# A hybrid transformer block on one core: two rows of inverse roots by transfers through DRAM instead of TensorE

## What is computed

```python
def rms_norm(x, g):
    xf = x.astype(jnp.float32)
    y = xf * lax.rsqrt(jnp.mean(xf * xf, axis=-1, keepdims=True) + EPS)
    return (y * g.astype(jnp.float32)).astype(x.dtype)

h = rms_norm(x, norm_mix_g[l])          # the input of the mixer
parts = jnp.split(h @ w_in, ...)        # all projections of the mixer
...
o = o * lax.rsqrt(jnp.mean(o * o, axis=-1, keepdims=True) + EPS) * norm_g    # end of the gated recurrence
```

## Time and profile before

| what | value |
|---|---|
| median of 3 runs | 923.76 us (923.7 to 924.11) |
| the profiled execution | 923.25 us, of which the span of the trace is 921.5 us |
| PE busy | 911.4 us, 99% of the span |
| DVE busy | 627.7 us, 68% |
| ACT busy | 404.8 us, 44% |
| POOL busy | 99.6 us, 11% |

### The profile page before, as it was taken

How to read it: one execution, slowest core, us unless ns; L and a number is a source line. 1 busy time by engine, 2 the same in 40 slices (tenths; PEclk the granted TensorE clock), 3 DMA queues, 4 the chain that set the end, 5 groups by cost and what they waited for, 6 DMA issues and landing times.

```text
span 921.5 us, 11738 instructions
## 1 busy us (share of the span) xinstructions
PE 911.4 (99%) x4590; PEld 757.4 (82%) x4590; DVE 627.7 (68%) x753; ACT 404.8 (44%) x472; POOL 99.6 (11%) x116
## 2 busy tenths in 40 slices
PE   8999999999999999999999999999999999999997
PEld 6888888888888888888888978888888888888886
DVE  6887654654778475656545758688777777777796
ACT  6463311331455532443344547433333433455674
POOL 0024342300322000000021004000000000000002
PEclk9999999999999999999999999999999999999999
DMA  7568899224798728433223224333355433255563
GB/s 219 184 159 241 226 245 237 80 71 103 181 224 201 194 80 209 124 102 125 92 99 130 70 70 138 91 92 91 91 142 139 129 91 91 91 173 201 185 200 143
DMA packets 137478, 132.48 MB, mean 144 GB/s; under 512 B 6651, under 2 KB 115295, under 8 KB 137183
## 3 DMA queue, kind: packets, MB, share of 16 engines
q1 hardware_dynamic: 127438, 108.62, 39.6%
q0 software_dynamic: 9856, 23.07, 11.5%
q10 hardware_dynamic: 144, 0.26, 0.1%
HBM read 122.23 MB, written 25.17 MB: 160 GB/s over the span
## 4 chain that ended last, share of the span: by engine, by line
PE 93%; DVE 4%; ACT 2%; DMA 0%; issue 0%; SPq 0%; DVEq 0%; ACTq 0%
PE ps L685 71%; PE ps L1210 6%; PE ps L1222 5%; PE ps L1086 5%; PE ps L739 1%; PE ps L1114 1%; DVE wL L1655 1%; DVE hgF L1655 1%; DMA xtok<-in_x 0%; PE ps L929 0%; ACT hgF L1262 0%; PE ps L895 0%; PE ps L855 0%; DVE hgG L1848 0%; PE ps L915 0%
## 5 line engine op out<-in xcount | busy, mean ns | idle before, releaser
L685 PE MATMUL ps<-hH,wH 128*128 128x512 f32 x784 | 307.9, 393 | 2.1 <-DVE wL L1655 1.2
L685 PE MATMUL ps<-hH,wL 128*128 128x512 f32 x784 | 305.2, 389 | 0.0
L685 PE MATMUL ps<-hL,wH 128*128 128x512 f32 x784 | 305.2, 389 | 0.0
L1655 DVE TENSOR_TENSOR wL<-raw,wH 128x2048 fp32r<-128x2048 f32 (+3 forms) x119 | 209.6, 1769 | 59.9 <-ACT wH L1262 59.7
L1262 ACT ACTIVATE wH<-raw 128x2048 fp32r<-128x2048 f32 (+3 forms) x119 | 176.0, 1488 | 136.6 <-PE ps L685 128.5
L685 PEld LDWEIGHTS ps<-hH,wH 128*128 128x128 f32 x784 | 147.2, 188 | 35.0 <-DVE wL L1655 2.6
L685 PEld LDWEIGHTS ps<-hH,wL 128*128 128x128 f32 x784 | 147.1, 188 | 31.0
L685 PEld LDWEIGHTS ps<-hL,wH 128*128 128x128 f32 x784 | 147.2, 188 | 29.7 <-issue 0.2
L1262 ACT ACTIVATE ca<-za,par 128x512 f32<-128x512 f32 x22 | 18.0, 818 | 100.4 <-DVE za L1655 100.4
L1662 DVE SCALAR_TENSOR_TENSOR ca<-za,par,ca 128x512 f32<-128x512 f32 x44 | 33.1, 752 | 25.6 <-ACT ca L1262 23.4
L1662 DVE SCALAR_TENSOR_TENSOR cu<-zu,par,cu 128x512 f32<-128x512 f32 x44 | 33.1, 752 | 25.5 <-ACT cu L1262 23.4
(11 more groups left out here) (326 smaller groups left out, 1449.1 us busy)
## 6 DMA issues: line engine op xcount, KB each, us to landing
raw<-in_w_in SPq DMA_DIRECT2D x57, 512.0 KB, 4.8
raw<-in_w_up SPq DMA_DIRECT2D x44, 512.0 KB, 4.9
t<-in_w_down POOLq DMA_DIRECT2D x66, 256.0 KB, 5.0
raw<-t SPq DMA_DIRECT2D x11, 768.0 KB, 4.7
raw<-in_w_branch SPq DMA_DIRECT2D x24, 256.0 KB, 4.8
t<-t POOLq DMA_DIRECT2D x22, 256.0 KB, 9.9
raw<-in_w_down SPq DMA_DIRECT2D x10, 512.0 KB, 4.2
raw<-in_w_out SPq DMA_DIRECT2D x8, 512.0 KB, 4.2
```

The costliest lines, as they stand in the source:

```text
L685: last = pe.matmul(out_ap, a, b, start=start and k + m == 0, stop=stop and m == 2 and k == len(terms) - 1)
L1655: q.sig(dve.tensor_tensor(out_ap, a, b, op), sem)
```

## The change

The two `rows_of` jobs on PE are gone. In their place POOL writes the small tile to a buffer `rows_dram` in DRAM, token by token, waits for that transfer, and reads the 512 numbers back as a row for all 128 partitions: `rstd` to `rstd_row`, and `statr` to a new tile `hgrow`. DVE's copy of bank 4 is gone, and its `job(14)` reads `hgrow` instead of the bank. DVE's `job(1)` (the blocks of cosines and sines) is now done in `job(0)`, and the wait for the row stands behind it.

```diff
+        hgrow = at("hgrow", T + 2 * KIB, [P, S])
...
+        rows_dram = nc.dram_tensor("rows_dram", (2, S), F32, kind="Internal").ap()
...
+            def row_by_dram(cols, r, row, done):
+
+                pool.dma_start(rows_dram[r].rearrange("(t p) -> p t", p=P), cols[:, 0:NT],
+                               allow_slow_non_contiguous=True).then_inc(done, 16)
+                pool.wait_ge(done, 16)
+                pool.dma_start(row[:, :], rows_dram[r].partition_broadcast(P)).then_inc(done, 16)
+
+            pool.wait_ge(rstd_ready, 1)
+            row_by_dram(rstd, 0, rstd_row, row_out)
...
                 pool.tensor_tensor(hgsq[:, 0, :], hgsq[:, 0, :], hgsq[:, h, :], ALU.add).then_inc(hg_sum, 1)
+            pool.wait_ge(hg_rs, 1)
+            row_by_dram(statr, 1, hgrow, hg_row)
...
-                if n == 0:
-                    pe.wait_ge(rstd_ready, 1)
-                    rows_of(rstd, 4, row_out)
-                elif n == 1:
+                if n == 1:
                     pe.wait_ge(wide_ready, 1)
...
-                elif n == 13:
-                    pe.wait_ge(hg_rs, 1)
-                    rows_of(statr, 4, hg_row)
...
                 if n == 0:
-                    dve.wait_ge(row_out, 1)
-                    copy(rstd_row[:, :], ps[:, 4, :])
-                    q.settle()
-                elif n == 1:
                     dve.wait_ge(fn_out, 3)
...
+                    dve.wait_ge(row_out, 2 * 16)
...
-                    dve.wait_ge(hg_row, 1)
+                    dve.wait_ge(hg_row, 2 * 16)
                     q.settle()
-                    tt(hgY[:, :, :], hgY[:, :, :], row4(ps[:, 4, :]), ALU.mult, hg_yf)
+                    tt(hgY[:, :, :], hgY[:, :, :], row4(hgrow[:, :]), ALU.mult, hg_yf)
```

More of the change, by code:

```diff
@@ L209, in hybrid_layer @@
         memst = at("memst", T + 2016, [P, 8])
-        assert T + 2048 <= nc.sbuf_usable_end
+        assert T + 4096 <= nc.sbuf_usable_end
         xtok = at("xtok", U_R, [P, NT, D])
@@ L739, in transposes @@
                     last = pe.transpose(out_ap, in_ap, ident[0:k, 0:k])
[L740 to L746, removed]
                 last.then_inc(done, 1)
```

## The result

The changed kernel takes **932.1 us** (median of 5 runs, 930.87 to 933.04); the kernel before, measured beside it, 923.7 (5 runs, 923.08 to 924.11). The ratio is 1.009, with a 95% interval of 1.0079 to 1.01: slower, by over four times what a measurement of this kernel can tell. The forecast was 923.3 with a range of 921.8 to 926.8. It was wrong in the sign and in the range.

A forecast was written before the change was run, and what follows sets the result against it. PE was taken as the bound: busy 99%, 93% of the last chain. Profiled 923.25 - 0.91 - 0.89 + 1.3 (PE's wait) = 922.75 us, or 923.3 against the runs' median; range 921.8 to 926.8.

The forecast's parts named there:

- PE's gain: Row matmuls behind slots 0 and 13 leave PE's path: 0.91 and 0.89 us, together 1.80 us.
- The place of the wait: Ahead of slot 2, PE waits for `wL`, which stands on DVE behind the read-out needing the row; 1.3 us.
- the forecast's own rule: At slot 2, the row must be in SBUF at 32.7 us; each microsecond later stops PE for one.
- the middle chain: ACT and DVE's gates from 48.48 us to `hgV`'s read-out at 82.15 start from PE's slot 2 and move with it.
- Rival (d): Middle chain does not start from PE's slot 2, so the first 0.9 us is lost: 924.2 us; chance 0.03.
- the price of the write: First row's 512 single floats, POOL to DRAM: 6.5 us, priced by the `sinks` loads of equal element count.
- The read: The 2 KB row read back from DRAM for 128 partitions: 3.0 us, up to 4.2.
- rival (b): At slot 2, the wait outweighs the removed matmuls: PE stands 5.9 us, 927.9 us; chance 0.25 beyond 0.2%.
- The second row: Behind slot 13, two transfers of 9.7 us are hidden before DVE's product of `hgY`: costed at nothing.
- rival (c): The second row takes more than 15 us after its roots; at 18 it costs some 2 us: 925.5; chance 0.02.
- the 10.9 us that hide the transfers: Time from the second row's roots to DVE reaching the `hgY` product, against 9.7 us for write and read.
- the estimate from the Trainium skill: Prices a GpSimd transfer at 2.0 us plus bytes over 436 GB/s: first row there at about 29 us.

The follow-up runs named there:

- the second row alone: Against the kernel before: only the second row goes through DRAM, the first still comes from PE's matmuls; 922.61 us against 923.5, ratio 0.999.
- issued by ScalarE: Against the turned kernel: the first row's four writes and its read are issued by ACT instead of POOL; 923.08 us, ratio 0.9994 to the kernel before.
- turned: Against the changed kernel: DVE turns the roots by 32x32 blocks, each row written as 16 runs of 128 bytes; 923.99 us, ratio 1.0007 to the kernel before.
- one moved line: Against the turned kernel: DVE makes `wL` of slot 2 before it waits for the row; 921.86 us against 923.39 for the kernel before, ratio 0.9981.

## Why the prediction was wrong

**Right.** PE's gain: 1.80 foreseen, 2.0 measured without the write, 0.9 for the second row alone. The place of the wait, and its way: DVE came to it at 32.1 (31.8 foreseen), PE was there at 36.8, the end of its transposes (36.3 foreseen for slot 2's start), held by `wL` of slot 2. From the row at 39.87 the forecast's own rule, each microsecond after 32.7 stops PE for one, gives 7.2; the trace shows 6.65, mostly because PE's work is 0.2 later and the end of its last transposes is not counted as waiting. That the middle chain moves with PE: 8.05 at 48 us, 8.04 at the slot behind `hgV`. Rival (d) is out.

**The step that failed: the price of the write.** I put it at 6.5 us, between 3.0 and 7.8, by the number of its elements alone, from four *loads* of `sinks`. It took 10.6, outside both bounds. The nearest row was near in the count and not in the kind: those elements were read from DRAM and went to 128 partitions, while these were all written into one 2 KB of DRAM. Written 64 or 256 bytes apart, the same 512 elements land in 6.1 and 6.2 us, in the middle of my bounds; as neighbours they pay 4.5 us more. My high end of 7.8 with 2 us more for the load beside it, 9.8, had no room for this. In the profiled execution the row came 5.9 us later than the 34.0 of the forecast: 4.1 for the write, 1.1 for the read, 0.4 because POOL's two waits took 0.3 each and not 0.1, and 0.2 for the start. PE waited 6.65 us instead of 1.3.

**The read** took 4.1 us, near the upper end of 4.2 (3.0 taken). In the other kernels a first row's read behind a write took 3.3 to 3.9; without a write, beside slot 3's load, it took 6.6. Write and read together: 15.0 with POOL's wait, where rival (b) decided from 11.9. So (b) was the right mechanism with a chance of 0.25; it priced the wait at 5.9. That its write, 7.8 + 2.1 = 9.9, lies near the 10.6 is partly luck: the 2.1 was for POOL's issue, which took 0.98, and the time was in the tail, which no rival had.

**The term that was missing: the clock.** No step had it, in the forecast or in (b). After 6.65 us of waiting slot 2 took 2.1 us more, 1.85 of it for the clock. With the wait of (b), 5.9, and these 2.1, (b) would have come to 930.0. This stop of PE was thus dearer than its length: 8.8 us for 6.65. The profiled executions beside each other:

| kernel | PE waits ahead of slot 2 | slot 2 takes |
|---|---|---|
| issued by ScalarE | 1.17 us | 11.19 us |
| pieces of 16 bytes | 1.27 | 11.19 |
| 64 bytes apart | 1.7 | 11.19 |
| 256 bytes apart | 1.91 | 12.83 |
| turned | 1.96 | 12.80 |
| SP's queue | 5.83 | 13.33 |
| changed kernel | 6.65 | 13.04 |

The table gives no threshold: it has one execution of each kernel, and the turned kernel's times say that the same stop cost the clock in three executions out of eleven.

**The second row** cost nothing in the forecast, against 9.7 us of transfers. They took 10.7 + 4.8 = 15.5, and the row came 16.1 us after the roots (188.69), just past the 15 that the forecast gave it. The product waited:

```profile
204.81 2.29 DVE L1656 TENSOR_TENSOR hgY<-hgY,hgrow 128x2048 f32<-128x2048 f32 x1 [4.37 <-DMA hgrow<-rows_dram]
```

```profile
207.16 0.88 PE L753 MATMUL ps<-ident,rqk 128*128 128x128 f32 x6 [0.18 <-DVE hgY L1656]
```

PE met 0.18 of it, at the place of the earlier trace rows. The condition of rival (c), over 15 us, was met, and it cost next to nothing, because my limit was 0.9 too low: the first row's 0.91 moves PE and DVE earlier, but the roots with them, so the limit was 15.9. The same slip stands in the 10.9 us that hide the transfers; the trace has 11.75 from the roots to DVE at the product. One more microsecond and the second row would have cost one.

**Two rules beside the traces.** By the estimate from the Trainium skill, DMA: Bandwidth & Descriptors, anatomy of one DMA, the row would have been there at 29 us; the trace has 39.87, and even the fastest whole write of a row took 4.2 us for 2 KB. The rule on GpSimd's descriptors beside VectorE's copies and tensor-scalar instructions (the Trainium skill, SBUF — State Buffer, who interferes with whom) had no test in the changed kernel, since DVE stood idle at 35.73. In the kernel with pieces of 16 bytes it had one: POOL's second issue began at 31.12, between cosine blocks that run on DVE to 32.1, and took 0.60 us against 0.57 beside an idle DVE: nothing was held there. With floats 64 bytes apart the same issue beside the same blocks took 0.57, but with floats 256 bytes apart 0.86, from 31.34 to 32.20, while the blocks ended at 32.08. Whether that one was held, and whether those blocks run in the mode that the Trainium skill means, no row says.

## What to carry to other kernels

Before you move work off the busiest engine into a round trip through DRAM, price the write in the form in which it falls into memory: single floats side by side were the dearest of the forms tried here. Look at what stands behind the new wait on the engine that waits: here 2.2 us of work that did not need the row stood behind it, and one moved line took off 2.1 us once the write was mended (the mending itself took off 8.1); what the line would be worth without the mending no run shows. And add to a stop of TensorE what its clock may take afterwards.

## What the runs showed of the hardware

- 512 writes of 4 bytes to one contiguous 2 KB in DRAM landed after 8.7 to 10.7 us, of which 4 to 6 us passed after the write's last packet, in the changed kernel with all DMA engines idle; 64 or 256 bytes apart they landed after 5.4 to 6.2 us, as 128 runs of 16 bytes after 4.2 to 5.9. It was the same on SP's queue (10.1).
- A 2 KB row read back for 128 partitions took 3.3 to 5.3 us, and 6.6 beside a load of 1 MB.
- In the profiled executions PE's granted clock stayed at 1.00 over waits of 1.17, 1.27 and 1.7 us and fell to 0.50 with waits of 1.91, 1.96, 5.83 and 6.65 us; in the first two of these it fell only when PE had been back at work for over 1 us, in the last two during the wait, and by its times the kernel with 1.96 us kept its clock in eight executions out of eleven; the slot at the fall took 12.80 to 13.33 us, where it takes 10.91 to 11.19 at 1.00.
